# Second expert matrix in row pairs: one 8 KB piece per partition, and column-pair reads in the turns

## The reference

```python
def _moe(h, w_router, b_router, w1, w3, w2):
    logits = (h @ w_router + b_router)
    top_l, top_e = lax.top_k(logits, MOE_TOPK)          # 2 of 8
    gates = jax.nn.softmax(top_l, axis=-1)
    ...
    def expert_group(args):
        xg, e = args
        return (jax.nn.silu(xg @ w1[e]) * (xg @ w3[e])) @ w2[e]
    # w1, w3: (8, 1024, 3584); w2: (8, 3584, 1024)
```

## Time and profile before

| | |
|---|---|
| median of 3 runs | 1953.8 us |
| the profiled execution | 1959.17 us, of which the span from first to last instruction is 1957.4 us |
| granted TensorE clock, mean over the span | 0.963 of 2.4 GHz |
| busy in the span: PE, DVE, ACT | 1818.5, 1503.4, 1200.0 us |
| the six small items | 690.7 to 1389.5 us; 114 us each after the first |
| the four large items | 1389.5 to about 1918.5 us; 132 us each |
| loads of expert units | 420 of 1 MB |

### The profile page before, as it was taken

One profiled execution on the slowest core, in us unless ns is written; L12 is line 12 of the kernel. 1 busy time (PEld: TensorE's weight loads), 2 busy tenths in 40 slices (PEclk: granted clock), 3 DMA queues, 4 the chain that ended last, 5 costly groups with the idle time before them and its releaser, 6 DMA issues.

```text
span 1957.4 us, 26569 instructions
## 1 busy us (share of the span) xinstructions
PE 1818.5 (93%) x9702; PEld 1445.5 (74%) x9702; DVE 1503.4 (77%) x1568; ACT 1200.0 (61%) x1115; POOL 18.2 (1%) x73
## 2 busy tenths in 40 slices
PE   6889799999999789999999999999999999999997
PEld 3766489999887756776767677676777787787775
DVE  3777464555798589898998989899788787887884
ACT  2233254444456168787888878788676677676673
POOL 2000000000000000000000000000000000000000
PEclk7988899999899779999999999999999999999998
DMA  9577777555825159999999999999999898998970
GB/s 328 204 276 274 278 256 219 176 172 179 248 87 200 62 204 373 385 393 395 378 386 388 381 383 392 397 378 388 346 334 367 287 356 320 332 355 316 334 286 23
DMA packets 221527, 579.23 MB, mean 296 GB/s; under 512 B 10478, under 2 KB 73398, under 8 KB 221437
## 3 DMA queue, kind: packets, MB, share of 16 engines
q1 hardware_dynamic: 220429, 573.98, 80.3%
q0 software_dynamic: 1024, 4.25, 0.7%
HBM read 574.79 MB, written 4.35 MB: 296 GB/s over the span
## 4 chain that ended last, share of the span: by engine, by line
PE 66%; DVE 17%; issue 8%; ACT 6%; SPq 2%; DMA 1%; DVEq 1%; ACTq 0%; PEldq 0%
PE banks L959 18%; PE banks L489 14%; DVE w_lo L1885 12%; PE banks L947 12%; PE banks L917 4%; ACT w_hi L1264 4%; PE banks L770 3%; PE banks L790 2%; PE banks L903 1%; PE banks L863 1%; PE banks L881 1%; PE banks L545 1%; DMA ring<-in_ada_w_dram 1%; PE banks L565 1%; PE banks L528 1%
## 5 line engine op out<-in xcount | busy, mean ns | idle before, releaser
L1885 DVE TENSOR_TENSOR w_lo<-ring,w_hi 128x2048 fp32r<-128x2048 f32 x420 | 947.1, 2287 | 156.9 <-ACT w_hi L1264 156.8
L1264 ACT CAST w_hi<-ring 128x2048 fp32r<-128x2048 f32 x420 | 798.3, 1911 | 278.5 <-PE banks L959 179.2
L959 PE MATMUL banks<-w_hi,x_s 128*128 128x512 f32 x672 | 280.8, 418 | 42.2 <-DVE w_lo L1885 37.6
L959 PE MATMUL banks<-w_hi,x_m 128*128 128x512 f32 x896 | 289.7, 400 | 2.2 <-DVE w_lo L1885 2.2
L947 PE MATMUL banks<-w_hi,g_buf 128*128 128x512 f32 x784 | 285.4, 405 | 4.7 <-DVE w_lo L1885 2.6
L959 PE MATMUL banks<-w_lo,x_s 128*128 128x512 f32 x672 | 267.1, 397 | 0.0
L947 PE MATMUL banks<-w_lo,g_buf 128*128 128x512 f32 x560 | 221.3, 395 | 0.0
L959 PEld LDWEIGHTS banks<-w_hi,x_s 128*128 128x128 f32 x672 | 127.0, 189 | 112.2 <-DVE w_lo L1885 83.1
L1417 DVE TENSOR_TENSOR w_lo<-ring,w_hi 128x1024 fp32r<-128x1024 f32 x124 | 143.8, 1203 | 82.0 <-ACT w_hi L1085 81.1
L959 PEld LDWEIGHTS banks<-w_hi,x_m 128*128 128x128 f32 x896 | 169.2, 189 | 43.1 <-DVE w_lo L1885 2.6
L1085 ACT CAST w_hi<-ring 128x1024 fp32r<-128x1024 f32 x124 | 121.5, 1031 | 129.7 <-PE banks L489 53.6
(11 more groups left out here) (377 smaller groups left out, 2047.2 us busy)
## 6 DMA issues: line engine op xcount, KB each, us to landing
ring<-in_moe_w_dram SPq DMA_DIRECT2D x420, 1024.0 KB, 6.9
ring<-in_ada_w_dram SPq DMA_DIRECT2D x48, 1024.0 KB, 6.5
ring<-in_ffn_w_dram SPq DMA_DIRECT2D x30, 1024.0 KB, 5.3
ring<-in_attn_w_qkv_dram SPq DMA_DIRECT2D x12, 1024.0 KB, 12.3
ring<-in_conv_w_pw_dram SPq DMA_DIRECT2D x12, 1024.0 KB, 12.2
ring<-in_cache_k_dram SPq DMA_DIRECT2D x16, 512.0 KB, 7.8
ring<-in_cache_v_dram SPq DMA_DIRECT2D x16, 512.0 KB, 6.1
ring<-in_attn_w_o_dram SPq DMA_DIRECT2D x4, 1024.0 KB, 7.9
```

The lines of the kernel that those rows point to most:

```text
L959: mm = pe.matmul(bk[:, b, :], x, y, start=(k == 0 and i == 0), stop=(k == KC - 1 and i == len(x_passes(k, hi, lo)) - 1), skip_group_check= ...
L1264: act.copy(w_unit(n)[0], ring[:, pos_of(n), :]).then_inc(ev("moe_hi_ready"), 1)
L1885: dve.tensor_tensor(lo, ring[:, pos_of(n), :], hi.bitcast(F32), ALU.subtract).then_inc(ev("moe_lo_ready"), 1)
```

## The change

The load of a w2 unit now puts two neighbouring rows of w2 on each partition: rows 2k and 2k + 1, which lie side by side in memory, so that each partition gets one piece of 8 KB in place of two of 4 KB. The same 256 rows land in the same slot. To match, the turns read every second column: block i takes the even (i even) or odd (i odd) columns of a stretch of 256, by the new helper `w2_columns`. The loads of w1 and w3 keep their form.

```diff
+        def w2_columns(i):
+            return slice(i // 2 * 2 * P + i % 2, (i // 2 + 1) * 2 * P, 2)
...
-                        mm = pe.matmul(t_b[:, b, i * SMALL:(i + 1) * SMALL], h_rows[:, b, i * P:(i + 1) * P], joint[:, :],
+                        mm = pe.matmul(t_b[:, b, i * SMALL:(i + 1) * SMALL], h_rows[:, b, w2_columns(i)], joint[:, :],
                                        start=True, stop=True)
...
-                            mm = pe.transpose(t_b[:, b, i * P:(i + 1) * P], h_rows[:, 0, (4 * b + i) * P:(4 * b + i + 1) * P], ident[:, :])
+                            mm = pe.transpose(t_b[:, b, i * P:(i + 1) * P], h_rows[:, 0, w2_columns(4 * b + i)], ident[:, :])
...
                 if kind == "w2":
                     f0 = j * 512 + part * 256
-                    src = moe_w2[0][bass.ds(e, 1), f0:f0 + 256, :].rearrange("o (k p) n -> p (o k) n", p=P)
+                    src = moe_w2[0][bass.ds(e, 1), f0:f0 + 256, :].rearrange("o (p k) n -> p (o k n)", k=2)
+                    sp.dma_start(ring[:, pos_of(s), :], src).then_inc(slot_sem[pos_of(s)], 16)
```

More of the change, by code:

```diff
@@ L2199, in expert_load @@
                     src = w[0][bass.ds(e, 1), part * rows:(part + 1) * rows, j * 512:(j + wide) * 512].rearrange("o (k p) n -> p (o k) n", p=P)
-                dst = ring[:, pos_of(s), :].rearrange("p (k n) -> p k n", n=src.shape[-1])
-                sp.dma_start(dst, src).then_inc(slot_sem[pos_of(s)], 16)
+                    dst = ring[:, pos_of(s), :].rearrange("p (k n) -> p k n", n=src.shape[-1])
+                    sp.dma_start(dst, src).then_inc(slot_sem[pos_of(s)], 16)
             def expert(e, w, s):
```

## The result

The changed kernel is slower: 1959.14 us median (1955.44 to 1963.55, 20 runs) against 1954.67 us (1952.06 to 1957.09, 20 runs). The ratio is 1.0022, 95% interval 1.0016 to 1.0029, so 3 to 6 us. The time lies inside the range that was given, but the forecast was "no change" and the change is clear of the noise.

The account below looks back on a forecast made before the run. DVE's work and its starving behind exposed PE turns were taken to bound small items, with loads off the path. Loads, small-item turns and large-item turns summed 0 + 0 + 0: 1953.8 us, range 1948 to 1962 us.

Parts of the forecast that it names:

- What bounds an item: Small items: DVE's 102.1 us of work plus 11.4 us starving; turns on PE exposed in full, loads off the path.
- The w2 loads: 140 of 420 loads in 8 KB pieces: 0 to 0.26 us gained per load, 0 for the kernel's time.
- The turns of the small items: 672 weight loads on PE reading every second column: taken as 0, at worst 74 us, 4 us between.
- that row: 8 weight loads at 608 to 610 us, 8 columns wide, stepping by 31 columns: 87 ns, as without a step.
- 4 and 74 us: Small items' 672 turn passes: 6 ns more each by L959's pace, or 110 ns more each if the time doubles.
- L959's pace of 8.8 bytes per ns: Read pace of L959 streaming 512 columns; over 1024 bytes it gives 116 ns a pass, 6 more than now.
- rival 1: Turns on PE: stepped weight load slow, 86 us if it doubles (0.05), a few microseconds in small form (0.06); chance 0.11.
- The turns of the large items: 112 passes on a full PE, so exposed: taken as 0, at worst another 110 ns each, 12 us.
- Rivals 2 to 4: Small items' loads set pace, 1932 us (0.07); 8 KB loads over 0.38 us slower (0.03); packets stay 4 KB (within forecast's 0.79).

Follow-up runs that it names:

- the loads alone: Changed kernel's 8 KB w2 loads, but turns reading neighbouring columns as in the kernel before: 1955.01 us against 1954.41, ratio 0.9998.
- The later steps: Kernel before with its old loads, turns reading every third, fourth or eighth column: 2032.46, 2088.5 and 2087.1 us (ratios 1.0402, 1.0684, 1.0681).

## Why the prediction was wrong

The mechanism was seen; a term of the sum was mis-sized.

- **What bounds an item** held. The loads are waited for by nobody, the turns lie on the chain in full; 3 x 0.19 + 0.09 = 0.66 us of longer turns are 0.6 to 0.8 us of longer item.
- **The w2 loads**: "0 for the time of the kernel" held, shown by the loads alone (0.9998). They are 3% faster (2.49 us for 2.56), not up to 10%: the 26.6 bytes per ns of the earlier trace rows came from pieces of another kind.
- **The turns of the small items** is the step that failed: "I take 0, being nearest to that row, and keep 4 and 74 us". It is the middle value: 672 passes x 6 ns = 4 us, as L959's pace of 8.8 bytes per ns gave it. The later steps show that the pace is not one by span, but at a step of two columns the span and the touched pieces of 16 bytes come to the same 116 ns. The wide turn of 3.71 us is just past the 3.7 us that the text had named as the sign of rival 1. The row that was chosen instead is of another kind: its loads are 8 columns wide, stand in front of 128 moving columns, and belong to transposes, and transposes pay another price: a step of eight takes the busy time of the large items' 112 transposes from 15.4 to 16.2 us, but that of the small items' 672 passes from 77.6 to 160.4. The text had worked out that for L917 the load sets the pace, and took its price from a place of which no row says so.
- The Trainium skill, "SBUF — State Buffer" (Specifications), has two hits on a line of 16 bytes as enough for full bandwidth. At two columns a line the runs show 116 ns in place of 110, so the rule is nearly right, and the measurement decides: 5% on a pass that is exposed is what made the kernel slower. That steps 4 and 8 cost the same agrees with its 16 bytes.
- **The turns of the large items** were taken at 0 as well and came out between the bounds of 0 and 12 us. Their weight loads show 208 ns, and an item is 0.4 to 0.5 us longer, 2 us in four items.
- The sum with measured terms is 6 x 0.7 + 4 x 0.45 = 6.0 us by the items, against 3 to 6 us by the runs (4.5 by the medians); the stretch before the items, which varies by some us from run to run, is not in it, and neither is the end of the program. In the profiles of the kernel before and of the changed one the first nine items are 5.5 us longer together (1101.3 against 1095.8), and the rest is 1.2 us shorter (169.7 against 170.9), which makes 4.3: a fall of the granted clock to 0.50 for 3.4 us, at 1934.3 us in the kernel before, is missing there. The version with columns set apart in the copies, which reads without a step, has the shorter end too (169.2), so it is not tied to the stepped read.
- **Rival 1** in its small form had 0.06 of the chance. Rivals 2 to 4 fell: the small items are not shorter, no copy on ACT waits for a load, and the packets are fewer.

## What to carry to other kernels

Before a layout is changed for the sake of transfers, look at how long each load lies before it is used: here 3.4 us at the least, so that faster loads could give nothing, while the price was paid at another engine that reads the data in the new order. When an operand must be taken with a step, let an engine do it that reads it for nothing (here ACT and DVE on the way out of PSUM) and keep the step out of the weight loads of short matmuls, in which the load sets the pace. And take the price of an unknown access from a row where that access is the slow part, not from one where something else may cover it.

## What the runs showed of the hardware that was not expected

- A 128-column float32 weight load in front of 64 moving columns: a pass takes 110, 116, 171, 229 and 234 ns at steps of 1, 2, 3, 4 and 8 columns, which from step 2 on is 1.8 ns for each piece of 16 bytes that it touches.
- At step 4 a turn took 7.34 us at a mean granted clock of 0.70 as well as at 0.82; at step 3 it took 5.46 us at 1.00 and 5.85 at 0.82.
- In front of a transpose the same load goes from 141 to 208 ns in the rows at steps 2 and 4, and the pass grows only from 277 to 293 ns.
- ACT's copy and DVE's product read PSUM with a step of two float32 columns in the same time as without (898 and 895 against 898 and 897 ns, 1078 against 1080).
- Long slow turns lower PE's granted clock in the small items from 1.00 to 0.89, which cost about 9 us an item at step 4, on top of the turns.
